# Layer norm in a two-block kernel: the mean from two products on TensorE, and the transposes of p before the inverse deviation

## The reference

```python
def layer_norm(x, g, b):
    mu = jnp.mean(xf, axis=-1, keepdims=True)
    xc = xf - mu
    var = jnp.mean(xc * xc, axis=-1, keepdims=True)
    y = xc * lax.rsqrt(var + LN_EPS) * g + b

h = layer_norm(DEEPNORM_ALPHA * x + mix, ln_g[i, 0], ln_b[i, 0])
h = layer_norm(DEEPNORM_ALPHA * h + sq_relu_mlp(h, mlp_w1[i], mlp_w2[i]), ln_g[i, 1], ln_b[i, 1])
x = h + jax.nn.sigmoid(h @ ple_w_gate[i]) * (p[i] @ ple_w_proj[i])
```

## Time and profile before

| what | value |
|---|---|
| median of three executions | 2374.68 us |
| the profiled execution's own time | 2377.4 us |
| its span, first to last instruction | 2375.6 us |
| mean granted TensorE clock | 0.992 |
| PE busy | 2301.7 us, 97% |
| DVE, ACT, POOL busy | 37%, 38%, 50% |

### The profile page before, as it was taken

One profiled execution on the slowest core, in us unless ns is written; L12 is line 12 of the kernel. 1 busy time (PEld: TensorE's weight loads), 2 busy tenths in 40 slices (PEclk: granted clock), 3 DMA queues, 4 the chain that ended last, 5 costly groups with the idle time before them and its releaser, 6 DMA issues.

```text
span 2375.6 us, 31683 instructions
## 1 busy us (share of the span) xinstructions
PE 2301.7 (97%) x12399; PEld 1853.8 (78%) x12399; DVE 886.9 (37%) x1447; ACT 891.2 (38%) x1256; POOL 1197.8 (50%) x1052
## 2 busy tenths in 40 slices
PE   8999999899999989999989999998999999999998
PEld 6777777688888777777768888876888888889897
DVE  5546554422222422666432122143554334313132
ACT  4343333623233443555362332445233224323233
POOL 4555666444444365888644444444312334555452
PEclk9999999999999999999999999999999999999999
DMA  4212221222232222212222223223211212233321
GB/s 152 71 61 82 71 71 54 77 92 88 91 103 88 89 90 60 63 54 63 90 78 92 88 88 106 88 71 83 75 51 37 71 54 72 89 89 94 101 80 62
DMA packets 237433, 188.94 MB, mean 80 GB/s; under 512 B 9279, under 2 KB 228860, under 8 KB 237196
## 3 DMA queue, kind: packets, MB, share of 16 engines
q1 hardware_dynamic: 233616, 183.66, 25.0%
q10 hardware_dynamic: 3708, 3.79, 0.5%
HBM read 185.30 MB, written 2.10 MB: 79 GB/s over the span
## 4 chain that ended last, share of the span: by engine, by line
PE 86%; POOL 6%; ACT 5%; issue 2%; DVE 1%; ACTq 0%; DMA 0%; DVEq 0%; SPq 0%; POOLq 0%
PE ps L2501 43%; PE ps L2703 12%; PE ps L1366 8%; PE ps L636 4%; PE ps L2590 2%; PE ps L2524 2%; POOL w_lo L1777 2%; POOL hdd L421 1%; POOL hdd L419 1%; PE ps L2564 1%; PE ps L2534 1%; PE ps L1333 1%; PE ps L1428 1%; PE ps L702 1%; PE ps L2834 1%
## 5 line engine op out<-in xcount | busy, mean ns | idle before, releaser
L1777 POOL TENSOR_TENSOR w_lo<-raw,w_hi 128x512 fp32r<-128x512 f32 (+2 forms) x760 | 897.2, 1213 | 840.9 <-ACT w_hi L1933 840.2
L1933 ACT ACTIVATE w_hi<-raw 128x2048 fp32r<-128x2048 f32 (+2 forms) x190 | 329.9, 1738 | 523.8 <-PE ps L2501 363.0
L2501 PE MATMUL ps<-a_hi,w_hi 128*128 128x512 f32 (+1 forms) x912 | 294.2, 354 | 8.5 <-POOL a_lo L842 4.5
L2501 PE MATMUL ps<-b_hi,w_hi 128*128 128x512 f32 x752 | 296.2, 394 | 3.2 <-POOL w_lo L1777 3.2
L2501 PE MATMUL ps<-b_hi,w_lo 128*128 128x512 f32 x752 | 297.9, 396 | 0.0
L2501 PE MATMUL ps<-b_lo,w_hi 128*128 128x512 f32 x752 | 296.2, 394 | 0.0
L2501 PE MATMUL ps<-a_lo,w_hi 128*128 128x512 f32 (+1 forms) x912 | 294.7, 355 | 0.0
L2501 PE MATMUL ps<-a_hi,w_lo 128*128 128x512 f32 (+1 forms) x912 | 294.0, 354 | 0.0
L2501 PEld LDWEIGHTS ps<-a_hi,w_hi 128*128 128x128 f32 x912 | 162.6, 190 | 37.0 <-issue 10.8
L2501 PEld LDWEIGHTS ps<-a_hi,w_lo 128*128 128x128 f32 x912 | 161.7, 191 | 24.6
L2501 PEld LDWEIGHTS ps<-a_lo,w_hi 128*128 128x128 f32 x912 | 161.1, 190 | 24.6
(11 more groups left out here) (371 smaller groups left out, 4177.1 us busy)
## 6 DMA issues: line engine op xcount, KB each, us to landing
raw<-in_mlp_w_dram SPq DMA_DIRECT2D x128, 512.0 KB, 4.3
raw<-in_w_up_dram SPq DMA_DIRECT2D x44, 512.0 KB, 5.0
raw<-in_ssd_w_in_dram SPq DMA_DIRECT2D x40, 512.0 KB, 4.8
raw<-in_hgrn_w_in_dram SPq DMA_DIRECT2D x48, 256.0 KB, 3.2
raw<-in_w_in_dram SPq DMA_DIRECT2D x24, 512.0 KB, 4.9
raw<-in_ssd_w_out_dram SPq DMA_DIRECT2D x16, 512.0 KB, 4.3
raw<-in_w_down_dram SPq DMA_DIRECT2D x16, 512.0 KB, 4.0
raw<-in_ple_w_gate_dram SPq DMA_DIRECT2D x12, 512.0 KB, 4.0
```

Of the source, the lines that this page charges most:

```text
L1777: last = nc.gpsimd.tensor_tensor(w_lo[:, slot, piece], raw[:, slot, i * q:(i + 1) * q], w_hi[:, slot, piece].bitcast(F32), ALU.subtract)
L1933: nc.scalar.activation(w_hi[:, slot, at:at + n], raw[:, slot, 0:n], ACT.Copy).then_inc(whi_ready, 1)
L2501: last = nc.tensor.matmul(ps[:, b + s, 0:nn], w[:, k, m * P:(m + 1) * P], v[:, k, c0 + s * nn:c0 + (s + 1) * nn], start=(k == 0 and first) ...
```

## The change

The running sum leaves out the last tile. TensorE makes the mean's sum from two products in the same bank: ones times the sum of seven tiles, which does not wait for the last tile, and ones times the last tile of `res`, which waits for VectorE to have added it. The transposes of p no longer wait for the inverse deviation, and the second half of p goes to bank 4, where the mean stood, in place of bank 5.

```diff
-        p_bank, proj_bank, gate_bank = (7, 5), (0, 1, 2, 3, 7, 0, 1, 2), (4, 5, 6)
+        p_bank, proj_bank, gate_bank = (7, 4), (0, 1, 2, 3, 7, 0, 1, 2), (4, 5, 6)
             def summed(m):
-                if m:
+                if 0 < m < KD - 1:
                     dve.wait_ge(free_dve, fd())
                     if m > 1:
                         own.wait()
                     ins = nc.vector.tensor_tensor(lv[:, 0:T], res[:, 0, 0:T] if m == 1 else lv[:, 0:T], res[:, m, 0:T],
                                                   ALU.add)
-                    if m < KD - 1:
+                    if m < KD - 2:
                         own.did(ins)
                     else:
                         ins.then_inc(sum_ready, 1)
-                with turns(dve, BLOCKS, {tile: 16, fd: 8, own.at: 6, b_at: KD}) as b:
+                with turns(dve, BLOCKS, {tile: 16, fd: 8, own.at: 5, b_at: KD}) as b:
             def ln_pe(n, between=None):
                 pe.wait_ge(sum_ready, n)
-                nc.tensor.matmul(bank[4], ones, lv[:, 0:T], start=True, stop=True).then_inc(mean_done, 1)
+                nc.tensor.matmul(bank[4], ones, lv[:, 0:T], start=True, stop=False)
+                pe.wait_ge(free_dve, fd())
+                nc.tensor.matmul(bank[4], ones, res[:, KD - 1, 0:T], start=False, stop=True).then_inc(mean_done, 1)
             def p_pe(i):
                 pe.wait_ge(s_ptok, 16 * (i + 1))
-                pe.wait_ge(rstd_ready, 2 * i + 1)
```

## The result

The changed kernel took 2382.71 us in the median of 13 executions (2376.66 to 2384.42), the kernel before beside it 2376.22 us (2374.27 to 2379.41). The ratio is 1.0018, with a 95% interval from 1.001 to 1.0025: slower by about 4 us. In two later sets the ratio was 1.0018 (1.0009 to 1.0028) and 1.001 (1.0001 to 1.0019). The forecast had +1.7 us, and the measured median lies above its range.

What follows compares the result with a forecast made beforehand. TensorE, busy 97% of the span with 86% of the chain, was taken to bound the kernel. Terms 1.74 + 0 + 0 + 0 + 0 = 1.74 us, put on the median 2374.68, gave 2376.4 us, range 2373.4 to 2378.6.

Steps and rivals of the forecast that it cites:

- The product in the full TensorE: Second and fourth norm: the added float32 product delays what follows by 0.87 us each, 1.74 us, bounds 0 and 2.26.
- The earlier mean at the first and third norm: Mean 0.7 and 1.3 us earlier, but ScalarE's table load is later: 0, bounds a gain of 2.0 us and 0.
- The transposes: Transposes of p before the MLPs, twice: already hidden behind the wait for ScalarE's `a_hi`, so 0, bounds -0.2 and 0.
- I take the clock as before: TensorE's granted clock at the changed pauses: 0, bounds -3.3 (both squares' losses recovered) and +3.4 (twice 1.7 lost anew).
- Rival (b): Pause behind early transposes drops the clock; each MLP's first 32 products lose 1.7 us: 2379.8 us, chance 0.07.
- The transfer onto the median of three executions: Whole kernel: the 1.74 us was put on the shown runs' median, 2374.68, not the profiled 2377.4: 2376.4 us.
- The range: Whole kernel: 2373.4 to 2378.6 us, holding the forecast, (c), and (a) but for its lower edge.
- The Trainium skill's rule on transposes: Moved transposes of p: they do not count as TensorE work for the clock as products do; term 0.

Runs made afterwards that it cites:

- second_fourth: Kernel before with two products for the mean at the second and fourth norm alone, transposes of p as before: ratio 1.0014 (1.0005 to 1.0023).
- first_third: Changed kernel with two products for the mean at the first and third norm alone, one at the others: ratio 1.0003 (0.9995 to 1.0012) against the kernel before.
- p_only: Kernel before with only the transposes of p moved behind the squares into bank 4, mean from one product: ratio 0.9994 (0.9985 to 1.0003).
- delay_two: Kernel before with two more float32 products, results overwritten, ahead of the second norm's mean: ratio 1.0002 (0.9994 to 1.0011).
- fill_squares: Kernel with two products at first and third norm alone, plus two overwritten products ahead of their squares: ratio 0.9984 (0.9976 to 0.9993) against the kernel before.
- one_fill: Kernel before, single-product mean, transposes moved, overwritten products filling the first and third norm's pauses: ratio 0.9995 (0.9986 to 1.0004).
- after_again: The changed kernel run again unaltered, for its spread and a profile; profiled execution 2381.24 us.
- after_third: The changed kernel run once more unaltered, for a profile of its upper group near 2383 us; profiled execution 2383.2 us.
- before_again: The kernel before run again unaltered, for a second profile and its spread: ratio 1.0005 (0.9996 to 1.0014); profiled execution 2374.59 us.

## Why the prediction was wrong

Step by step:

- The product in the full TensorE, 1.74 us: right. 0.86 and 0.87 in the chain; +1.5 ± 0.3 us outside the clock's loss where it stands alone (second_fourth), +2.1 ± 0.3 in the changed kernel.
- The earlier mean at the first and third norm, 0: right in its reason. VectorE's centred tiles began 0.73 us earlier and ScalarE's square did not. first_third, which holds this and the moved transposes, is within its interval of no change.
- The transposes, 0 within -0.2: right within what was measured; p_only is 0.9994 (0.9985 to 1.0003), its mean 1.3 us below. The pause that the move makes was put at 2.3 us, though its rows give 1.50 + 0.55 = 2.05; it measured 2.25, and the clock did not fall there in the changed kernel's profiles.
- "I take the clock as before: 0, bounds -3.3 and +3.4". This is the step that failed, a term put at nothing. It measured +1.7 ± 0.7 us in the mean of 37 executions, the larger part of the 2.1 ± 0.5 us by which the whole exceeds 1.74. The term's bounds held it, but the range stopped at 2378.6 us, and I reasoned only about the pauses that the change touches. The upper profile shows 5 us of added loss in the second block, where nothing was changed; delay_two shows a loss that is 2.6 ± 1.0 us lower with a delay alone.
- Rival (b) came nearest to the measured time (5.1 us over its median; measured about 4 by the ratio), for another reason. Its pause does lower the clock in some executions (fill_squares), not in the three profiles of the changed kernel, and where it did, at the first MLP, it was covered.
- The transfer onto the median of three executions, 2374.68. In 13 it was 2376.22 us, and over 116 the mean is 2377.17. The executions lie in groups (near 2374.5, 2377.3 and 2379.3 us), and two of the three had been of the lowest. That took 1.5 us of the miss of 6.3. The groups go with the granted clock (0.993, 0.992 and 0.990), so this is the clock's term once more.
- The range was built from bounds around one execution; it held neither the spread of the kernel before nor a shift of it.
- The Trainium skill's rule on transposes (TensorE: Matmul & The Clock Gate, Part 4: PE-mode transpose), that they do not count for the clock as products do, was left at a term of 0, and that stood. What the runs add: in fill_squares TensorE did 1.04 us of transposes and stood for 2.25 us, and the clock was 0.50 from 446.4 us on; in the changed kernel's profiles it did and stood the same, and the clock stayed at 1.00. No run here separates the transposes from the moment.

What stays open: why the loss is +1.7 for the changed kernel and -2.6 for a pure delay of the same length, put at one norm in place of two. The profiles show that it lies in different stages by the execution; why the changed kernel has more executions in its upper group is not shown, and nothing here predicts the loss for a given delay.

## What to carry to other kernels

Where TensorE has short pauses, read more than one profile before the clock is taken as a constant, and split each time into what the clock took and the rest; a change of 1 or 2 us can be drowned or doubled by pauses hundreds of us downstream. An instruction put into a full engine costs its row, and one taken from an engine whose successor waits for something else gives nothing: look at what stands 0.01 us ahead of the next step. A pause that cannot be removed can be filled with products that nobody reads: with the mean from two products at the first and the third norm this gave 4.1 us below the kernel before, with the single product (one_fill) nothing that can be told.

## What was not expected of the hardware

The kernel before, with the same pauses ahead of them, runs the squares of its first norm in 7.13 or in 8.83 us, by the execution. Its executions fall into groups 2 to 3 us apart with granted clocks of about 0.993, 0.992 and 0.990. The length of a wait alone does not tell whether the clock falls: in the first MLP, at about 471 us, it fell to 0.50 behind waits of 2.04 (before), 1.82 (after_again) and 1.78 us (after_third), and stayed at 1.00 behind 2.04 (before_again) and 1.98 us (the changed kernel's first profile, and delay_two). And two float32 products, 1.72 us, added to a TensorE that is busy for 97% of the span left the time at 1.0002 (0.9994 to 1.0011) of what it was.
